# Unit 25 as three single-pass products, whole-unit low halves and an earlier mean in a two-layer decoder trunk

## Chip, core and metric

One NeuronCore of one Trainium2 chip runs the whole program. The metric is the device time of one execution in microseconds (us). The kernel before took 326.81 us (median of 3 runs, 326.73 to 327.3).

## What is computed

256 tokens of width 1024 pass through two residual layers. The change lies in layer 0:

```
def pool_conv_layer(x, norm_g, w_in, pool_w, pool_scale, conv_w, conv_b, cn_g, cn_b, w_out):
    h = rms_norm(x, norm_g)
    proj = jnp.einsum('bsd,de->bse', h, w_in)
    a, bv, bg, z = jnp.split(proj, [A_W, A_W + B_W, A_W + 2 * B_W], axis=-1)
    pooled = multiscale_pool(a.reshape(B, S, POOL_GROUPS, POOL_CH))
    ya = jnp.einsum('bsgc,gce->bsge', pooled, pool_w).reshape(B, S, A_W) * pool_scale
    u = bv * jax.nn.sigmoid(bg)
    u = lax.conv_general_dilated(u, conv_w[:, None, :], ...) + conv_b   # 31 causal taps
    yb = jax.nn.silu(layer_norm(u, cn_g, cn_b))
    y = jnp.concatenate([ya, yb], axis=-1) * jax.nn.silu(z)
    return jnp.einsum('bse,ed->bsd', y, w_out)          # x = x + this
```

Layer 1 is causal attention with a gate and its own two projections; nothing in its code changes. All inputs and outputs are float32.

## The kernel before

Channels lie on the 128 partitions, tokens on the free axis. The weights come as 49 units of 128 x 2048 float32 (1 MB each), loaded by SP into a ring of four slots (`raw`); unit n goes into slot n % 4 once unit n - 4 has been used up there. PE works through the units in order. Units 0 to 15 and 17 to 20 are layer 0's input projection, 16 is the pooling map, 21 to 24 (`OA`) and 25 to 28 (`OB`) are the two halves of layer 0's output projection, 29 to 32 (`Z1`) begin layer 1.

A unit is multiplied in one of two ways. In a **native** unit the float32 operands go to PE as they are; each of the 16 products of 256 columns is then two passes in the trace. Any other unit is cut: ACT copies each half (128 x 1024) rounded into `w_hi` (`cut_hi`, L466), DVE subtracts that from the raw half into `w_lo` (`cut_lo`, L750), and PE makes three single passes for a product (`product`, L1087 to L1089): high by high, high by low, low by high. Four units (`ADDED`) get their low part another way: ACT writes minus the high half into `w_lo` (L469), and a DMA issued by POOL adds the raw half to it (L431). The activations are split into high and low in the same way.

`w_hi` and `w_lo` have three slots in rotation, and a fourth that unit 22 uses first and the split activations `yb_hi` and `yb_lo` of the `OB` units afterwards.

While PE goes through units 1 to 20, DVE and ACT also make the 31 taps of the convolution, by a plan that the program works out in advance: for each unit n a list of taps (L864 one tile on DVE, L868 the addition of a product that ACT made at L557 or L537). In each such slot DVE first cuts the low halves of unit n + 2, then does its taps. After the last taps the order around the change is this:

- DVE folds the eight channel tiles to one for the layer norm's mean (L881, three instructions); PE multiplies that by a matrix of ones (L1213) in the middle of unit 23, at the place that `MEAN_AT` names: unit index, half, product.
- DVE subtracts the mean (L888), ACT squares (L474), DVE folds (L775), PE sums (L1167) in unit 24, at the place that `SUM2_AT` names.
- ACT takes the root (L478), DVE inverts it (L781), normalises (L931), ACT applies silu (L618), DVE gates with silu(z) (L936). The result `yb` is read by unit 25 as float32, and by units 26 to 28 in high (L625) and low (L941) parts.
- PE does units 25 and 26, then `closing` takes units 27 and 28 together, product row by product row, and counts each of four PSUM banks off as it is finished (`bank_closed`), so that DVE can add the residual (L969).

Each wait is a count on a semaphore; an engine executes its instructions strictly in the order in which they are written.

```
NATIVE = frozenset((0, 9, 16, 23, 25))
MEAN_AT = 2, 0, 5
SUM2_AT = 3, 0, 2
...
dve.wait_ge(hi_cut, 2 * s + half + 1)     # cut_lo: each half waits for its own high half
```

Of the kernel before, what the change touches and what calls it, by code (L numbers as in the profile page):

```python
# [17 lines left out]
F32 = mybir.dt.float32  # L18
F32R = mybir.dt.float32r
ALU = mybir.AluOpType  # L20
# [32 lines left out]
O1 = [45 + i for i in range(4)]  # L53
NU = 49

NATIVE = frozenset((0, 9, 16, 23, 25))
EARLY_ADDED = (10,)
ADDED = EARLY_ADDED + (21, 22, 24)
SPARE = 22
WARM = 12  # L60
RAW = 4
# [17 lines left out]
    return sum(1 for m in range(n) if m not in NATIVE)  # L79


def low_cuts(n):

    return sum(1 for m in range(n) if m not in NATIVE and m not in ADDED)


CUTS = [n for n in range(NU) if n not in NATIVE]
# [154 lines left out]
CONV_PLAN, TILE_DONE, PRODUCT_USED, LATE_FROM, FOLDED = conv_plan()  # L242


MEAN_AT = 2, 0, 5
SUM3_AT = 5
SUM2_AT = 3, 0, 2
EARLY = (BG[0],), (Z1[0], Z1[1], Z1[2])


def hybrid_trunk(nc, xT, w, vec, const, out):
    with ExitStack() as ctx:
# [3 lines left out]
        def sem(name):  # L256
            return ctx.enter_context(nc.semaphore(name))
# [80 lines left out]
        hi_cut, lo_cut = sem("hi_cut"), sem("lo_cut")  # L338
        minus_hi = sem("minus_hi")
        lo_added = [[sem(f"lo_added{n}{half}") for half in range(2)] for n in ADDED]  # L340
        unit_done = sem("unit_done")
        first_square, sq_ready, folded = sem("first_square"), sem("sq_ready"), sem("folded")
        rms_sum = sem("rms_sum")
# [25 lines left out]
        def column(c, n=1):  # L369
            return V_[:, c:c + n]  # L370
# [19 lines left out]
        @block.sync  # L390
        def _(sp):
            for i in range(2):
                sp.dma_start(X[:, 4 * i:4 * i + 4, :], xT[:, 4 * i:4 * i + 4, :]).then_inc(x_in[i], 16)
            for n in range(NU):
                m = n - RAW
                if m >= 0:
                    if m in NATIVE:
                        sp.wait_ge(unit_done, m + 1)
                    elif m in ADDED:
                        for half in range(2):  # L400
                            sp.wait_ge(lo_added[ADDED.index(m)][half], 16)
                    else:
                        sp.wait_ge(lo_cut, 2 * low_cuts(m) + 2)
                sp.dma_start(raw[:, n % RAW, :], w[stored_at(n), :, :]).then_inc(raw_in[n % RAW], 16)
                if n == 3:
                    sp.dma_start(C_[:, :], const).then_inc(const_in, 16)
            for m in range(4):
                sp.wait_ge(x_updated, 4 + m + 1)
                sp.dma_start(out[:, 2 * m:2 * m + 2, :], X[:, 2 * m:2 * m + 2, :]).then_inc(stored, 16)
            sp.wait_ge(stored, 64)  # L410
# [3 lines left out]
        def _(pool):  # L414
# [30 lines left out]
            for n in ADDED:  # L445
                if n not in EARLY_ADDED:
                    added_low(n)

            for r in range(8):
                pool.wait_ge(qk_ss, r + 1)  # L450
# [6 lines left out]
        def _(act):  # L457
            def cut_hi(n, parts=(0, 1)):

                if n >= NU or n in NATIVE:  # L460
                    return
                act.wait_ge(raw_in[n % RAW], 16 * (n // RAW + 1))
                if slot_free(n):
                    act.wait_ge(unit_done, slot_free(n))
                for half in parts:
                    nc.scalar.copy(halves(w_hi, cut_slot(n), half), halves(raw, n % RAW, half)).then_inc(hi_cut, 1)  # L466
                    if n in ADDED:
                        act.wait_ge(hi_cut, 2 * cut_index(n) + half + 1)
                        nc.scalar.mul(halves(w_lo, cut_slot(n), half), halves(w_hi, cut_slot(n), half).bitcast(F32),  # L469
                                      -1.0).then_inc(minus_hi, 1)  # L470
# [133 lines left out]


            act.wait_ge(ya_ready, 4)
            cut_hi(OB[1])
            for m in range(4):
                act.wait_ge(centred, m + 1)
                square(1, m, V)  # L610
            prime(ACT.Sqrt)
            cut_hi(OB[0])
            take_root(bank[2], 2)
            prime(ACT.Silu)
            for m in range(5):
                for c in (2 * m, 2 * m + 1) if m < 4 else ():
                    act.wait_ge(normed, c + 1 if m == 0 else 2 * m + 2)
                    nc.scalar.activation(V[:, c, :], V[:, c, :], ACT.Silu, bias=column(CBETA + c),  # L618
                                         scale=column(CG + c)).then_inc(swished, 1)
                if m >= 3:  # L620
                    cut_hi(OB[2], (m - 3,))
                if m >= 1 and OB[m - 1] not in NATIVE:
                    act.wait_ge(yb_ready, 2 * m)
                    act.wait_ge(unit_done, released(SPARE))
                    nc.scalar.copy(yb_hi[:, 2 * m - 2:2 * m, :], SZ[:, KD + 2 * m - 2:KD + 2 * m, :]).then_inc(ybhi_ready, 1)  # L625
            for n in range(OB[3], Z1[1]):
                cut_hi(n)

# [111 lines left out]

        @block.vector
        def _(dve):
            def cut_lo(n, parts=(0, 1)):

                if n >= NU or n in NATIVE or n in ADDED:
                    return
                s = cut_index(n)
                for half in parts:
                    dve.wait_ge(hi_cut, 2 * s + half + 1)
                    nc.vector.tensor_tensor(halves(w_lo, cut_slot(n), half), halves(raw, n % RAW, half),  # L750
                                            halves(w_hi, cut_slot(n), half).bitcast(F32), ALU.subtract).then_inc(lo_cut, 1)
# [146 lines left out]
            for n in range(1, OA[0] + 1):  # L898
# [5 lines left out]
                    value = bank[m % 4][:, :].rearrange("p (c t) -> p c t", c=2)  # L904
                    nc.vector.tensor_tensor(U[:, 2 * i:2 * i + 2, PAD:PAD + S], value, SG2, ALU.mult).then_inc(u_ready, 1)
                if n < OA[0] and n != A[3]:
                    cut_lo(n + 2)
                if m in A:
                    window_sums(m - A[0])
                if m in ZA:  # L910
# [4 lines left out]
                                            YP[:, 2 * i:2 * i + 2, :], ALU.mult).then_inc(ya_ready, 1)  # L915
                taps(n)
                if n == A[3]:
                    cut_lo(n + 2)
# [4 lines left out]

            centre()
            fold(1, 0, 4)
            cut_lo(OB[1], (0,))
            take_inverse(2)
            dve.wait_ge(sq_ready, 8)

# [9 lines left out]
            def low_yb(m):  # L939
                dve.wait_ge(ybhi_ready, pairs_cut(OB, m + 1))  # L940
                nc.vector.tensor_tensor(yb_lo[:, 2 * m:2 * m + 2, :], SZ[:, KD + 2 * m:KD + 2 * m + 2, :],  # L941
                                        yb_hi[:, 2 * m:2 * m + 2, :].bitcast(F32), ALU.subtract).then_inc(yblo_ready, 1)

            dve.wait_ge(sz_ready, 8)
            assert OB[0] in NATIVE
            normalise(0, 1)
            normalise(1, 2)
            gate_yb(0, 1)
            normalise(2, 4)
            gate_yb(1, 2)  # L950
            normalise(4, 6)
            gate_yb(2, 4)
            normalise(6, 8)
            low_yb(1)
            cut_lo(OB[1], (1,))
            for m in (2, 3):
                gate_yb(2 * m, 2 * m + 2)
                cut_lo(OB[2], (m - 2,))
                low_yb(m)
            for n in range(OB[3], Z1[1]):  # L960
                cut_lo(n)

# [120 lines left out]
        def _(pe):  # L1083
# [149 lines left out]

            for i in range(2):
                n = OB[i]
                if n not in NATIVE:
                    pe.wait_ge(yblo_ready, pairs_cut(OB, i + 1))
                for kt in range(2):
                    if n in NATIVE:
                        pe.wait_ge(yb_ready, 2 * i + kt + 1)  # L1240
# [5 lines left out]
            def closing(units, y, first_tile, acc, ready):  # L1246

                pe.wait_ge(ready[0], ready[1])
                for n in units:
                    assert n not in NATIVE  # L1250
                    arrived(n, 1)
                for m in range(KD):
                    for u, n in enumerate(units):
                        for kt in range(2):
                            last = out_product(n, kt, m, y, first_tile + 2 * u + kt, acc, False, u == len(units) - 1 and kt == 1)
                        if m == KD - 1 and u == 0 and len(units) == 2:
                            last.then_inc(unit_done, 1)
                    if m % 2 == 1 and m < KD - 1:
                        last.then_inc(bank_closed, 1)
                last.then_inc(unit_done, 1)  # L1260

            closing(OB[2:], (yb_hi, yb_lo), 4, 4, (yblo_ready, pairs_cut(OB, 4)))


            for n in Z1:
# [190 lines left out]
```

## Time and profile before

| | us |
|---|---|
| median of 3 runs | 326.81 |
| the profiled execution's own time | 326.94 |
| span of its trace | 325.1 |
| PE busy (2238 instructions) | 320.4 (99% of the span) |
| DVE busy (484) | 261.6 (80%) |
| ACT busy (440) | 236.8 (73%) |
| POOL busy (58) | 51.1 (16%) |

Busy time is the time in which an engine executed something. PE's instructions overlap in the pipeline, so its pace is read from the distance between starts, not from the duration of one. Between the profiled time and the span lie 1.84 us around the program; the profiled execution is 0.13 us above the median.

### The profile page before, as it was taken

To read this page: it belongs to the slowest core of one execution; us is meant where nothing else is said; L and a number is where in the kernel's file an instruction comes from. 1 tells how busy PE (TensorE), PEld (TensorE's weight loads), DVE (VectorE), ACT (ScalarE), POOL (GpSimd) and SP (SyncE) were. 2 spreads that over 40 slices of the span, in tenths; PEclk is the share of its full clock that TensorE was granted. 3 is DMA by queue.
4 is the path that set the end of the run, shared out by engine and by line. 5 is a ranking of instruction groups with operands and counts; after the bars stand their busy time and mean duration, and the time that the engine had idled before them with its cause. 6 is when DMAs were issued, how large, how long until landed. Compare 5 with 4: busy or idle time off the path is not lost.

```text
span 325.1 us, 5846 instructions
## 1 busy us (share of the span) xinstructions
PE 320.4 (99%) x2238; PEld 294.2 (90%) x2238; DVE 261.6 (80%) x484; ACT 236.8 (73%) x440; POOL 51.1 (16%) x58
## 2 busy tenths in 40 slices
PE   8999999999999999999999999999999999999995
PEld 8899999999999999998999999988877777778885
DVE  2799989999999999998895899746555877758533
ACT  4787999997999998997766588434666767566630
POOL 0040024422225112211000000004500231400000
PEclk9999999999999999999999999999999999999999
DMA  7988478979999599986639234871645323200003
GB/s 267 419 325 335 139 255 231 203 150 344 339 331 221 100 369 346 211 268 132 255 134 422 94 132 144 355 276 31 227 138 188 129 97 119 109 2 0 2 1 131
DMA packets 12844, 64.80 MB, mean 199 GB/s; under 512 B 1424, under 2 KB 1552, under 8 KB 6544
## 3 DMA queue, kind: packets, MB, share of 16 engines
q1 hardware_dynamic: 8064, 53.78, 44.3%
q0 software_dynamic: 4608, 10.49, 17.4%
q8 instruction: 18, 0.29, 0.3%
q10 hardware_dynamic: 144, 0.15, 0.2%
q14 instruction: 10, 0.08, 0.1%
HBM read 52.88 MB, written 1.05 MB: 166 GB/s over the span
## 4 chain that ended last, share of the span: by engine, by line
PE 99%; DVE 0%; POOL 0%; issue 0%; POOLq 0%
PE bank L1087 27%; PE bank L1088 26%; PE bank L1089 26%; PE bank L1147 4%; PE bank L1121 4%; PE bank L1198 2%; PE bank L1302 2%; PE bank L1329 2%; PE bank L1315 2%; PE bank L1155 2%; PE bank L1167 1%; PE bank L1281 1%; DVE X L969 0%; PE bank L1213 0%; POOL ones L415 0%
## 5 line engine op out<-in xcount | busy, mean ns | idle before, releaser
L750 DVE TENSOR_TENSOR w_lo<-raw,w_hi 128x1024 fp32r<-128x1024 f32 x80 | 95.1, 1220 | 15.1 <-ACT w_hi L466 14.8
L466 ACT CAST w_hi<-raw 128x1024 fp32r<-128x1024 f32 x88 | 88.5, 1047 | 5.7 <-PE bank L1089 4.1
L1087 PE MATMUL bank<-h_hi,w_hi 128*128 128x256 f32 x304 | 86.6, 285 | 0.0
L1089 PE MATMUL bank<-h_hi,w_lo 128*128 128x256 f32 x304 | 86.0, 283 | 0.0
L1088 PE MATMUL bank<-h_lo,w_hi 128*128 128x256 f32 x304 | 86.0, 283 | 0.0
L1088 PEld LDWEIGHTS bank<-h_lo,w_hi 128*128 128x128 f32 x304 | 58.3, 192 | 0.1
L1087 PEld LDWEIGHTS bank<-h_hi,w_hi 128*128 128x128 f32 x304 | 58.3, 192 | 0.1
L1089 PEld LDWEIGHTS bank<-h_hi,w_lo 128*128 128x128 f32 x304 | 58.3, 192 | 0.0
L1087 PE MATMUL bank<-ya_hi,w_hi 128*128 128x256 f32 x160 | 46.9, 293 | 0.0
L1089 PE MATMUL bank<-ya_hi,w_lo 128*128 128x256 f32 x160 | 45.2, 283 | 0.0
L1088 PE MATMUL bank<-ya_lo,w_hi 128*128 128x256 f32 x160 | 45.2, 282 | 0.0
L864 DVE SCALAR_TENSOR_TENSOR scratch<-scratch,params 128x256 f32<-128x256 f32 x104 | 42.6, 477 | 0.2
L1087 PE MATMUL bank<-w_hi,h_hi 128*128 128x512 f32 x96 | 39.2, 408 | 0.0
L1088 PE MATMUL bank<-w_lo,h_hi 128*128 128x512 f32 x96 | 37.6, 391 | 0.0
L1089 PE MATMUL bank<-w_hi,h_lo 128*128 128x512 f32 x96 | 37.5, 391 | 0.0
L557 ACT ACTIVATE scratch<-scratch,params 128x256 f32<-128x256 f32 x80 | 33.7, 502 | 0.5 <-DVE scratch L868 0.5
L440 POOL DMA_DIRECT2D side_v<-side_ring x24 | 21.1, 907 | 73.9 <-ACT side_ring L537 52.9
L1087 PEld LDWEIGHTS bank<-ya_hi,w_hi 128*128 128x128 f32 x160 | 30.6, 191 | 2.0 <-issue 1.7
L1088 PEld LDWEIGHTS bank<-ya_lo,w_hi 128*128 128x128 f32 x160 | 30.6, 191 | 0.1
L1089 PEld LDWEIGHTS bank<-ya_hi,w_lo 128*128 128x128 f32 x160 | 30.6, 191 | 0.0
L868 DVE TENSOR_TENSOR scratch<-scratch 128x512 f32<-128x512 f32 x40 | 26.2, 684 | 0.4
L1087 PEld LDWEIGHTS bank<-w_hi,h_hi 128*128 128x128 f32 x96 | 18.0, 188 | 5.6 <-issue 2.3
(107 smaller groups left out, 507.8 us busy)
## 6 DMA issues: line engine op xcount, KB each, us to landing
raw<-w SPq DMA_DIRECT2D x49, 1024.0 KB, 6.3
side_v<-side_ring POOLq DMA_DIRECT2D x24, 256.0 KB, 7.1
w_lo<-raw POOLq DMA_DIRECT2D x8, 512.0 KB, 7.4
X<-xT SPq DMA_DIRECT2D x2, 512.0 KB, 5.3
out<-X SPq DMA_DIRECT2D x4, 256.0 KB, 2.6
consts<-const SPq DMA_DIRECT2D x1, 290.0 KB, 13.6
params<-vec ACTq DMA_DIRECT2D x1, 149.0 KB, 5.0
```

Source lines behind the costliest of these rows:

```text
L440: pool.dma_start(side_v[:, pair, item % 2, :, :], side_home(pair, item), accum_op=ALU.add).then_inc(side_added[pair][item % 2], 16)
L466: nc.scalar.copy(halves(w_hi, cut_slot(n), half), halves(raw, n % RAW, half)).then_inc(hi_cut, 1)
L557: last = nc.scalar.mul(product_home(product)[:, i, :], U[:, c, k:k + S], column(CW + TAPS * c + k))
L750: nc.vector.tensor_tensor(halves(w_lo, cut_slot(n), half), halves(raw, n % RAW, half), halves(w_hi, cut_slot(n), half).bitcast(F32), ALU.s ...
L864: nc.vector.scalar_tensor_tensor(V[:, c, :], U[:, c, k:k + S], column(CW + TAPS * c + k), V[:, c, :], ALU.mult, ALU.add).then_inc(tap, 1)
L868: nc.vector.tensor_tensor(V[:, c:c + 2, :], V[:, c:c + 2, :], product_home(product), ALU.add).then_inc(tap, 1)
L1087: nc.tensor.matmul(dst, wh, ah, start=start, stop=False, skip_group_check=True)
L1088: nc.tensor.matmul(dst, wh, al, start=False, stop=False, skip_group_check=True)
L1089: return nc.tensor.matmul(dst, wl, ah, start=False, stop=stop, skip_group_check=True)
L1121: last = nc.tensor.matmul(dst, wr, (H if n else H0)[:, k, :], start=start, stop=stop, skip_group_check=True)
L1147: return nc.tensor.matmul(dst, wr, SZ[:, (KD if n in OB else 0) + tile, :], start=start and m % 2 == 0, stop=stop, skip_group_check=True)
L1155: nc.tensor.matmul(bank[7][:, 0:P], ones[:, :], ones[:, :], start=True, stop=True, skip_group_check=True)
```

## The change

Unit 25 leaves the set of native units. Its first low half is made by ACT and an added DMA on POOL's queue, its second by DVE; its activations are split too. For the units 3 to 20 that DVE cuts, one subtraction of 128 x 2048 takes the place of two of 128 x 1024, and waits for both high halves. The mean and the sum of squares each stand two products earlier in PE's order. The high and low parts of the first two `yb` tiles are made one tile at a time. Unit 26 is cut later on ACT and DVE, one half after the other. The last two `OB` units are taken bank by bank, first unit 27's four products for the bank and then unit 28's.

```
-NATIVE = frozenset((0, 9, 16, 23, 25))
+NATIVE = frozenset((0, 9, 16, 23))
+HALF_ADDED = 25
-MEAN_AT = 2, 0, 5
+MEAN_AT = 2, 0, 3
-SUM2_AT = 3, 0, 2
+SUM2_AT = 3, 0, 0
...
@@ SP: slot of unit 25 for unit 29
-                        sp.wait_ge(lo_cut, 2 * low_cuts(m) + 2)
+                        if m == HALF_ADDED:
+                            sp.wait_ge(half_added, 16)
+                        sp.wait_ge(lo_cut, low_cuts(m, 1))
@@ POOL, after the last added unit
+            n = HALF_ADDED
+            pool.wait_ge(minus_hi, 2 * len(ADDED) + 1)
+            pool.dma_start(halves(w_lo, cut_slot(n), 0).bitcast(F32), halves(raw, n % RAW, 0),
+                           accum_op=ALU.add).then_inc(half_added, 16)
@@ ACT, cut_hi
-                    if n in ADDED:
+                    if n in ADDED or n == HALF_ADDED and half == 0:
@@ ACT, after the gated ya
-            cut_hi(OB[1])
+            cut_hi(OB[0], (0,))
             for m in range(4):
                 act.wait_ge(centred, m + 1)
                 square(1, m, V)
+            cut_hi(OB[0], (1,))
             prime(ACT.Sqrt)
-            cut_hi(OB[0])
             take_root(bank[2], 2)
             prime(ACT.Silu)
+            cut_hi(OB[1], (0,))
...
+                if m == 0:
+                    high_yb(0, 1)
+                    high_yb(1, 2)
+                if m == 1:
+                    cut_hi(OB[1], (1,))
                 if m >= 3:
                     cut_hi(OB[2], (m - 3,))
+                if m >= 2:
+                    high_yb(2 * m - 2, 2 * m)
@@ DVE
+            def cut_lo_whole(n):
+                if n in NATIVE or n in ADDED:
+                    return
+                dve.wait_ge(hi_cut, 2 * cut_index(n) + 2)
+                nc.vector.tensor_tensor(w_lo[:, cut_slot(n), :], raw[:, n % RAW, :], w_hi[:, cut_slot(n), :].bitcast(F32),
+                                        ALU.subtract).then_inc(lo_cut, 2)
...
-                    cut_lo(n + 2)
+                    cut_lo_whole(n + 2)
...
-            cut_lo(OB[1], (0,))
+            cut_lo(OB[0], (1,))
             take_inverse(2)
...
@@ PE
-                    pe.wait_ge(lo_cut, 2 * low_cuts(n) + half + 1)
+                elif n == HALF_ADDED and half == 0:
+                    pe.wait_ge(half_added, 16)
+                else:
+                    pe.wait_ge(lo_cut, low_cuts(n, half))
...
+                    pe.wait_ge(yblo_ready, kt + 1 if i == 0 else 3)
...
-            closing(OB[2:], (yb_hi, yb_lo), 4, 4, (yblo_ready, pairs_cut(OB, 4)))
+            for b in range(4):
+                for u, n in enumerate(OB[2:]):
+                    if b == 0:
+                        pe.wait_ge(yblo_ready, 4 + u)
+                    for kt in range(2):
+                        if b == 0:
+                            arrived(n, kt)
+                        for m in (2 * b, 2 * b + 1):
+                            last = out_product(n, kt, m, (yb_hi, yb_lo), 4 + 2 * u + kt, 4, False, u == 1 and kt == 1)
+                    if b == 3 or u == 1:
+                        last.then_inc(unit_done if b == 3 else bank_closed, 1)
```

The order on DVE changes at the cuts of units 19 and 20 and after the root. First the end of the taps, before; the two rows of L750 are the low halves of units 19 and 20:

```order
79 L750 TENSOR_TENSOR w_lo<-raw,w_hi 128x1024 x2
80 L914 TENSOR_TENSOR scratch<-scratch 128x512
81 L864 SCALAR_TENSOR_TENSOR scratch<-scratch,params 128x256 x6
82 L861 TENSOR_TENSOR scratch<-scratch,side_v 128x512
83 L914 TENSOR_TENSOR scratch<-scratch 128x512
```

The same place after the change:

```order
79 L768 TENSOR_TENSOR w_lo<-raw,w_hi 128x2048
80 L942 TENSOR_TENSOR scratch<-scratch 128x512
81 L892 SCALAR_TENSOR_TENSOR scratch<-scratch,params 128x256 x6
82 L889 TENSOR_TENSOR scratch<-scratch,side_v 128x512
83 L942 TENSOR_TENSOR scratch<-scratch 128x512
```

Only the size of the subtraction differs there; nothing is moved past it, and the taps that follow are the same.

DVE after the inverse of the root, before (L931 normalise, L936 gate, L941 low part of yb, L750 low half of a unit: 26, 27, 27, then 28 and 29):

```order
102 L931 TENSOR_TENSOR scratch<-scratch,rinv 128x256 x2
103 L936 TENSOR_TENSOR scratch<-scratch 128x256
104 L931 TENSOR_TENSOR scratch<-scratch,rinv 128x512
105 L936 TENSOR_TENSOR scratch<-scratch 128x256
106 L931 TENSOR_TENSOR scratch<-scratch,rinv 128x512
107 L936 TENSOR_TENSOR scratch<-scratch 128x512
108 L931 TENSOR_TENSOR scratch<-scratch,rinv 128x512
109 L941 TENSOR_TENSOR w_lo<-scratch,w_hi 128x512
110 L750 TENSOR_TENSOR w_lo<-raw,w_hi 128x1024
```

And after the change (L959 normalise, L964 gate, L969 low part of yb, L778 low half of a unit, here 26 twice):

```order
102 L959 TENSOR_TENSOR scratch<-scratch,rinv 128x256 x2
103 L964 TENSOR_TENSOR scratch<-scratch 128x256 x2
104 L969 TENSOR_TENSOR w_lo<-scratch,w_hi 128x256
105 L959 TENSOR_TENSOR scratch<-scratch,rinv 128x512
106 L969 TENSOR_TENSOR w_lo<-scratch,w_hi 128x256
107 L778 TENSOR_TENSOR w_lo<-raw,w_hi 128x1024
108 L964 TENSOR_TENSOR scratch<-scratch 128x512
109 L959 TENSOR_TENSOR scratch<-scratch,rinv 128x512
110 L778 TENSOR_TENSOR w_lo<-raw,w_hi 128x1024
111 L969 TENSOR_TENSOR w_lo<-scratch,w_hi 128x512
112 L959 TENSOR_TENSOR scratch<-scratch,rinv 128x512
```

Two low parts of one tile and both halves of unit 26 now stand between the gates, and the last normalise comes behind them.

PE around the mean, before (L1147 products of unit 23, L1213 the mean):

```order
966 L1147 MATMUL bank<-scratch,raw 128x256 x6
967 L1213 MATMUL bank<-scratch,ones 128x256
968 L1147 MATMUL bank<-scratch,raw 128x256 x10
```

And after the change:

```order
966 L1179 MATMUL bank<-scratch,raw 128x256 x4
967 L1245 MATMUL bank<-scratch,ones 128x256
968 L1179 MATMUL bank<-scratch,raw 128x256 x12
```

The mean stands behind four products of unit 23 in place of six.

## Rows read from the trace of the kernel before

**Rows 1.** The page: busy time, and the chain that ended last by engine.
```profile
PE 320.4 (99%) x2238; PEld 294.2 (90%) x2238; DVE 261.6 (80%) x484; ACT 236.8 (73%) x440; POOL 51.1 (16%) x58
...
PE 99%; DVE 0%; POOL 0%; issue 0%; POOLq 0%
```

**Rows 2.** Timeline of PE, units 24 to 26: start, duration, instruction, count.
```profile
159.20 0.28 PE L1089 MATMUL bank<-ya_hi,w_lo 128*128 128x256 f32 x1
159.32 7.07 PE L1147 MATMUL bank<-scratch,raw 128*128 128x256 f32 x32
166.04 0.47 PE L1087 MATMUL bank<-w_hi 128*128 128x256 f32 x1
166.34 0.28 PE L1088 MATMUL bank<-w_lo,w_hi 128*128 128x256 f32 x1
```

**Rows 3.** Stretches: length, busy PE, PEld, DVE, ACT, POOL (instructions), clock, DMA share, GB/s.
```profile
60.00:104.00 44.00, 44.00 (x343) 43.17 (x343) 43.10 (x72) 41.38 (x82) 13.10 (x16) 1.00 1.01 273
104.00:134.00 30.00, 30.00 (x227) 29.17 (x227) 29.83 (x57) 28.09 (x49) 6.25 (x8) 1.00 0.90 258
```

**Rows 4.** Timeline of DVE, cuts of units 19 and 20; idle time before it in brackets.
```profile
115.17 2.36 DVE L750 TENSOR_TENSOR w_lo<-raw,w_hi 128x1024 fp32r<-128x1024 f32 x2 [0.17 <-ACT w_hi L466]
117.44 1.89 DVE L868 TENSOR_TENSOR scratch<-scratch 128x512 f32<-128x512 f32 x3
...
120.71 2.36 DVE L750 TENSOR_TENSOR w_lo<-raw,w_hi 128x1024 fp32r<-128x1024 f32 x2
122.99 0.68 DVE L914 TENSOR_TENSOR scratch<-scratch 128x512 f32<-128x512 f32 x1
```

**Rows 5.** Timeline of ACT: pooling results, then the high halves of units 19 and 20.
```profile
111.16 3.03 ACT L602 ACTIVATE scratch<-bank,params 128x256 f32<-128x256 f32 x8 [0.43 <-PE bank L1198]
114.03 2.04 ACT L466 CAST w_hi<-raw 128x1024 fp32r<-128x1024 f32 x2
...
119.61 2.02 ACT L466 CAST w_hi<-raw 128x1024 fp32r<-128x1024 f32 x2
```

**Rows 6.** Timeline of DVE, cuts of units 5 and 7.
```profile
30.59 2.36 DVE L750 TENSOR_TENSOR w_lo<-raw,w_hi 128x1024 fp32r<-128x1024 f32 x2
...
42.91 2.36 DVE L750 TENSOR_TENSOR w_lo<-raw,w_hi 128x1024 fp32r<-128x1024 f32 x2 [1.08 <-ACT w_hi L466]
```

**Rows 7.** Timeline of ACT: high halves of unit 5, last pair's first taps.
```profile
29.52 1.98 ACT L466 CAST w_hi<-raw 128x1024 fp32r<-128x1024 f32 x2
...
60.62 1.08 ACT L569 ACTIVATE scratch<-scratch,params 128x256 f32<-128x256 f32 x2
```

**Rows 8.** Timeline of DVE: first low part of ya, mean's folds.
```profile
132.53 0.68 DVE L895 TENSOR_TENSOR ya_lo<-scratch,ya_hi 128x512 fp32r<-128x512 f32 x1
...
145.24 2.41 DVE L881 TENSOR_TENSOR scratch<-scratch 128x1024 f32<-128x1024 f32 x3 [0.23 <-DVE scratch L868]
```

**Rows 9.** Timeline of PE: start of unit 21, unit 23 with the mean, sum in 24.
```profile
133.99 0.28 PE L1087 MATMUL bank<-ya_hi,w_hi 128*128 128x256 f32 x1
...
145.51 2.75 PE L1147 MATMUL bank<-scratch,raw 128*128 128x256 f32 x12
148.10 0.59 PE L1213 MATMUL bank<-scratch,ones 128*128 128x256 f32 x2
...
154.11 0.70 PE L1167 MATMUL bank<-scratch,ones 128*128 128x256 f32 x2
```

**Rows 10.** Groups of PE's weight loads, ya by w_lo: mean ns of one.
```profile
L1089 PEld LDWEIGHTS bank<-ya_hi,w_lo 128*128 128x128 f32 x160 | 30.6, 191 | 0.0
```

**Rows 11.** Timeline of ACT: the root, released by the sum.
```profile
154.85 0.47 ACT L478 ACTIVATE root<-bank,eps 128x256 f32<-128x256 f32 x1 [1.08 <-PE bank L1167]
```

**Rows 12.** Timeline of DVE: first gate of yb, low halves of unit 28.
```profile
158.24 0.42 DVE L936 TENSOR_TENSOR scratch<-scratch 128x256 f32<-128x256 f32 x1 [0.33 <-ACT scratch L618]
...
168.35 2.35 DVE L750 TENSOR_TENSOR w_lo<-raw,w_hi 128x1024 fp32r<-128x1024 f32 x2
```

**Rows 13.** DMA issues on POOL's queue: count, KB each, median us to landing.
```profile
w_lo<-raw POOLq DMA_DIRECT2D x8, 512.0 KB, 7.4
```

More of the change, by code:

```diff
@@ L79, in cut_index, with low_cuts @@
     return sum(1 for m in range(n) if m not in NATIVE)
-def low_cuts(n):
-    return sum(1 for m in range(n) if m not in NATIVE and m not in ADDED)
+def low_cuts(n, half):
+    whole = sum(2 for m in range(n) if m not in NATIVE and m not in ADDED)
+    return whole + half + 1 - (n > HALF_ADDED or n == HALF_ADDED and half == 1)
 CUTS = [n for n in range(NU) if n not in NATIVE]
@@ L340, in hybrid_trunk @@
         lo_added = [[sem(f"lo_added{n}{half}") for half in range(2)] for n in ADDED]
+        half_added = sem("half_added")
         unit_done = sem("unit_done")
@@ L610, in _, with high_yb @@
                 square(1, m, V)
+            cut_hi(OB[0], (1,))
             prime(ACT.Sqrt)
-            cut_hi(OB[0])
             take_root(bank[2], 2)
             prime(ACT.Silu)
+            cut_hi(OB[1], (0,))
+            def high_yb(a, b):
+                act.wait_ge(yb_ready, b)
+                nc.scalar.copy(yb_hi[:, a:b, :], SZ[:, KD + a:KD + b, :]).then_inc(ybhi_ready, 1)
+            act.wait_ge(unit_done, released(SPARE))
             for m in range(5):
@@ L619, in _ @@
                                          scale=column(CG + c)).then_inc(swished, 1)
+                if m == 0:
[3 more added lines that the diff above has]
+                    cut_hi(OB[1], (1,))
                 if m >= 3:
                     cut_hi(OB[2], (m - 3,))
[L622 to L625, printed above, removed]
+                if m >= 2:
+                    high_yb(2 * m - 2, 2 * m)
             for n in range(OB[3], Z1[1]):
@@ L917, in _ @@
                 if n == A[3]:
-                    cut_lo(n + 2)
+                    cut_lo_whole(n + 2)
                 if n == OA[0]:
@@ L937, in gate_yb, with low_yb @@
                                         V[:, a:b, :], ALU.mult).then_inc(yb_ready, b - a)
[L939 to L942, printed above, removed]
+            def low_yb(a, b, copies):
+                dve.wait_ge(ybhi_ready, copies)
+                nc.vector.tensor_tensor(yb_lo[:, a:b, :], SZ[:, KD + a:KD + b, :], yb_hi[:, a:b, :].bitcast(F32),
+                                        ALU.subtract).then_inc(yblo_ready, 1)
             dve.wait_ge(sz_ready, 8)
-            assert OB[0] in NATIVE
             normalise(0, 1)
@@ L948, in _ @@
             gate_yb(0, 1)
+            gate_yb(1, 2)
+            low_yb(0, 1, 1)
             normalise(2, 4)
-            gate_yb(1, 2)
+            low_yb(1, 2, 2)
+            cut_lo(OB[1], (0,))
+            gate_yb(2, 4)
             normalise(4, 6)
-            gate_yb(2, 4)
+            cut_lo(OB[1], (1,))
+            low_yb(2, 4, 3)
             normalise(6, 8)
-            low_yb(1)
-            cut_lo(OB[1], (1,))
             for m in (2, 3):
@@ L958, in _ @@
                 cut_lo(OB[2], (m - 2,))
-                low_yb(m)
+                low_yb(2 * m, 2 * m + 2, m + 2)
             for n in range(OB[3], Z1[1]):
@@ L1235, in _ @@
                 n = OB[i]
-                if n not in NATIVE:
-                    pe.wait_ge(yblo_ready, pairs_cut(OB, i + 1))
                 for kt in range(2):
-                    if n in NATIVE:
-                        pe.wait_ge(yb_ready, 2 * i + kt + 1)
+                    pe.wait_ge(yblo_ready, kt + 1 if i == 0 else 3)
                     arrived(n, kt)
@@ L1244, in _ @@
                 last.then_inc(unit_done, 1)
[L1246 to L1260, printed above, removed]
-            closing(OB[2:], (yb_hi, yb_lo), 4, 4, (yblo_ready, pairs_cut(OB, 4)))
+            for b in range(4):
[9 more added lines that the diff above has]
+                        last.then_inc(unit_done if b == 3 else bank_closed, 1)
             for n in Z1:
```

## The prediction

> **What bounds the kernel now.** I read the page first: PE is busy for 99% of the span, and the chain that ended last is 99% PE [rows 1]. So a change gains only what it takes out of PE's instruction stream, and loses whatever it makes PE wait. Second, the timeline of PE gives its pace: a single-pass product starts every 0.12 us, and unit 25, native, takes from 159.32 to 166.04; the pass after it is followed 0.30 later in place of 0.12 [rows 2]. Third, the stretches: the clock stands at 1.00, the higher of its two levels (2.4 GHz), and beside PE, DVE is almost as full, 43.10 of 44 us and 29.83 of 30 up to the end of the taps [rows 3]. DVE makes the mean that PE needs in unit 23, so DVE's timeline is where a wait would come from.
>
> **The change, part by part.**
>
> *Unit 25.* Native it costs 6.72 from its first pass to the next unit's, and 0.18 more by the slow step behind it: 6.90 [rows 2]. As a cut unit it has 48 passes of 0.12: 5.76. PE's stream loses **1.14 us**. Bounds of this: 1.0 if the slow step is no part of it, 1.2 with the rounding of the starts.
>
> *Whole low halves.* Fifteen units (3 to 8, 11 to 15, 17 to 20) have two subtractions joined. Two halves take 2.28 (120.71 to 122.99 [rows 4]). Three operations of 512 columns stand (1.89 - 0.68) / 2 = 0.605 apart [rows 4], so 512 columns more are 0.535, and a whole unit is 1.14 + 1.07 = 2.21: 0.07 less. Fifteen times is 1.0 us of DVE, all of it hidden behind PE, worth something only if the mean comes sooner. Against it, the joined one waits for both high halves. For unit 19 DVE starts its first half at 115.17, after waiting 0.17 for ACT [rows 4]; ACT's second half ends at 114.03 + 2.04 = 116.07 [rows 5]. ACT has worked without a gap since PE's pooling products released it at 111.16 [rows 5], so that end does not move forward. The whole subtraction starts at about 116.11, with 0.04 from release to start (the sum's end, 154.11 + 0.70, to the root at 154.85 [rows 9, 11]), and ends 2.21 later at 118.32; what stood at 117.44 is **0.88 late**. For unit 20 ACT's second half ends at 119.61 + 2.02 = 121.63 [rows 5], DVE arrives at about 121.6, and nothing is won back: the row of 122.99 goes to 123.88. From there to the last fold DVE has no idle time but 0.23 of its own, and every instruction there stays as it is, so the lateness passes on whole.
>
> It can be more than that. Unit 5 is the first case: both halves start at 30.59 [rows 6], ACT's second ends at 29.52 + 1.98 = 31.50 [rows 7], which makes DVE 0.88 late with no idle time to take it back but the 1.08 ahead of unit 7 [rows 6]. ACT itself waits for DVE's u before the first taps of the last pair (60.62 [rows 7]); these go later, with them the next high halves, and DVE then waits for these. Each later cut pays back 0.07 only. So at unit 19 DVE can come with more than 0.88 of its own. I take **1.1**, with ends 0.88 (units 19 and 20 alone) and 1.5 (one more such wait, two thirds of it kept).
>
> Here the Trainium skill speaks on both sides ("Perfetto Trace Analysis", Optimizing Scalar/DVE Operations). It puts about 60 ns of overhead on each DVE operation in SBUF and advises larger operations where the engine is saturated; by that alone DVE would be 15 x 60 ns = 0.9 us early (an estimate from that page), and nothing would be lost. The same section advises breaking instructions up where an engine that isn't saturated causes bubbles on others. The 0.07 of the rows agrees with the first; but the rows of units 19 and 20 show a producer half a unit behind, so I go by them.
>
> *First output unit.* Unit 21 needs the first low part of ya, which ends at 132.53 + 0.68 = 133.21 [rows 8]. At 1.1 late that is 134.31; a start of PE from a standstill costs 0.04 and a weight load of 0.19 [rows 10]: 134.54 against 133.99 [rows 9]. PE waits about 0.55. It isn't added, since the mean's wait is counted from the same plan.
>
> *The mean.* The last fold ends at 145.24 + 2.41 = 147.65 [rows 8], the mean's product runs at 148.10: 0.45 to spare. Twelve passes from 145.51 make 0.216 each [rows 9]; with four passes fewer ahead of it the mean is due at 148.10 - 0.86 = 147.24. Even with DVE as before, the fold would end after that. With 1.1 late it ends at 148.75, PE starts at 148.98: PE is **1.74 behind** its plan (1.52 and 2.14 at the ends).
>
> *From the mean to unit 25.* Before, the sum follows the mean by 6.01 (148.10 to 154.11 [rows 9]), with ACT held by two copies of unit 26. After, the sum's place in PE's order is 1.2 earlier but there are four passes more of unit 23 between: 0.43 + 12 x 0.43 + about 0.7 = 6.3, so DVE and ACT have as long as before; ACT's added copy and negation (1.05 each) fall into its wait for the mean. Nothing added. From the sum to unit 25 there are 15 products in place of 13: 5.21 + 0.72 = 5.93. The chain takes 158.24 + 0.42 - 154.11 = 4.55 to the first gate [rows 9, 12]; then 0.2 for a half of unit 26 cut ahead of silu on ACT, 0.3 because the second silu goes before the copy, 0.5 copy, 0.42 subtraction, 0.1 between them: 6.0 with PE's start. It just fits: **0.1**, ends 0 and 0.3. The added DMA is issued when ACT's negation is done, near 150, and lands 7.4 later [rows 13], 3 us before its use; its cover is that distance.
>
> *Units 26 to 28.* DVE ends unit 28's low halves 168.35 + 2.35 - 154.11 = 16.6 after the sum [rows 9, 12]. It gets two low parts (0.34 each) and a half of unit 26 (1.14) more, that is 18.4 without waits; ACT gets two halves of unit 26 and two small copies, about 2.7, and the last normalise now stands behind a low part that waits for ACT, so silu of the last tiles, the cut of unit 27 and DVE's subtraction of it all come later, by about 1.3. That makes 19.7. PE wants unit 28's second half at 5.93 + 2 x 5.76 + 6 products of 0.36 = 19.6, less 0.2 for the load. **0.4**, ends 0 and 0.8. The bank by bank order itself has the same products, and closes banks at the same products: 0. Later stages all wait for PE, and shift with it.
>
> Sum: 1.74 - 1.14 + 0.1 + 0.4 = +1.1 on the profiled 326.94, that is 328.0; this execution is 0.13 above the median, so the median would go from 326.81 to 327.9.
>
> **The rivals.** *Short waits.* DVE's lateness is the 0.88 of units 19 and 20 only, and the closing units are covered: 1.52 - 1.14 = +0.4, 327.2. For it: DVE idles 1.08 ahead of unit 7's cut [rows 6], which swallows what unit 5 loses. Against it: the stretch after that has hardly any idle time [rows 3]. *No wait at the mean: faster.* If the joined subtractions really bring DVE forward, the mean is in time and unit 25's 1.14 is kept: 325.7. It decides at the last fold: it must end by about 147.0, 0.65 earlier than before. For it: 1.0 us of DVE is saved on paper, and ACT could run ahead where its own waits for DVE shrink. Against it: ACT's stretch from 111.16 to 121.63 is released by PE [rows 5], so the cuts of units 19 and 20 can't come sooner. *The change does nothing that shows*, since the conversion is off the path: excluded by the chain, which is PE throughout [rows 1].
>
> **How the numbers follow.** A measurement of this kernel tells some 0.2% (0.65 us) from no change. The forecast gets 0.62, short waits 0.22, faster 0.13, something longer than all these 0.03. The predicted time is 327.9. Its own ends are +0.4 and +2.1 (1.52 or 2.14, less 1.14, and 0 or 1.1 behind it): 327.2 to 328.9. The range goes from 326.7, to take in short waits whose mean is nearly in time, to 328.9. Slower by over 0.2%: 0.62; within: 0.25 (short waits, and the low edge of the forecast); faster: 0.13.
>
> **What would show it.** Right: PE's timeline with a gap ahead of the mean and a smaller one at unit 21; the waits list with PE waiting for DVE's folds; DVE idle ahead of the cuts of units 19, 20 and 5; unit 25 as 48 passes of 0.12 in 5.76. Wrong: the last fold before 147.3, the mean's product at 147.24 without a gap, or a gap at unit 25 or in units 27 and 28 that is larger than the one at the mean.

## The result, and the profile after

The changed kernel takes 328.32 us (median of 5 runs, 328.16 to 328.84); the kernel before took 327.18 us in the same comparison (5 runs, 326.73 to 327.3). The ratio is 1.0044, 95% interval 1.003 to 1.0058: slower by 0.4%, some 1.4 us (1.0 to 1.9). The forecast was 327.9 us, slower by 1.1. The profiled execution took 328.32 us with a span of 326.4, against 326.94 and 325.1.

The page of the kernel after, the rows that answer to [rows 1]:

```profile
PE 319.7 (98%) x2254; PEld 294.0 (90%) x2254; DVE 262.2 (80%) x472; ACT 241.0 (74%) x445; POOL 51.9 (16%) x59
...
PE 89%; DVE 3%; DMA 3%; ACT 3%; issue 1%; POOL 0%; ACTq 0%; POOLq 0%
```

PE's busy time fell by 0.7 us although the kernel became longer, and the chain that ended last, 99% PE before, now runs for 9% through DVE, DMA and ACT. PE's waits say for what (us in total, times, longest):

```profile
PE bank L1117 <- DMA w_lo<-raw: 1.6, 1, 1.6
PE bank L1187 <- POOL eps L421: 1.0, 1, 1.0
PE bank L1117 <- DVE w_lo L778: 0.3, 1, 0.3
```

The 1.0 is the start of the program and stood there before too. New are a wait for an added transfer and one for DVE. The timeline of PE shows where (start, duration, instruction; idle time in brackets):

```profile
133.74 0.28 PE L1119 MATMUL bank<-h_hi,w_lo 128*128 128x256 f32 x1
135.59 0.35 PE L1117 MATMUL bank<-ya_hi,w_hi 128*128 128x256 f32 x1 [1.57 <-DMA w_lo<-raw]
...
147.18 1.89 PE L1179 MATMUL bank<-scratch,raw 128*128 128x256 f32 x8
148.95 0.67 PE L1245 MATMUL bank<-scratch,ones 128*128 128x256 f32 x2
...
155.00 0.61 PE L1199 MATMUL bank<-scratch,ones 128*128 128x256 f32 x2
...
160.85 0.28 PE L1117 MATMUL bank<-w_hi 128*128 128x256 f32 x1
...
166.49 0.28 PE L1119 MATMUL bank<-w_hi,w_lo 128*128 128x256 f32 x1
...
173.69 0.28 PE L1119 MATMUL bank<-w_hi,w_lo 128*128 128x256 f32 x1
174.23 0.35 PE L1117 MATMUL bank<-w_hi 128*128 128x256 f32 x1 [0.26 <-DVE w_lo L778]
...
174.89 0.28 PE L1119 MATMUL bank<-w_hi,w_lo 128*128 128x256 f32 x1
175.27 0.38 PE L1117 MATMUL bank<-w_hi 128*128 128x256 f32 x1
```

Passes start 0.12 apart, so unit 21 was due at 133.74 + 0.12 = 133.86 and began at 135.59: PE loses 1.73 us there. It then reaches the mean 13.36 later, at 148.95, without a wait that the page lists (the kernel before takes 148.10 - 133.99 = 14.11 [rows 9] with four passes more, so 14.11 - 0.86 = 13.25 for as many). Unit 25's 48 passes run from 160.85 to 166.49 + 0.12 = 166.61, that is 5.76. In unit 28 PE stands twice, 174.23 - 173.81 = 0.42 and 175.27 - 175.01 = 0.26, together 0.68.

DVE's timeline, at the cuts of units 19 and 20 (L768, to be held against [rows 4]), the first low parts of ya and the folds ([rows 8]), and the closing units:

```profile
116.55 2.28 DVE L768 TENSOR_TENSOR w_lo<-raw,w_hi 128x2048 fp32r<-128x2048 f32 x1
118.75 1.88 DVE L896 TENSOR_TENSOR scratch<-scratch 128x512 f32<-128x512 f32 x3
...
121.95 2.28 DVE L768 TENSOR_TENSOR w_lo<-raw,w_hi 128x2048 fp32r<-128x2048 f32 x1
124.15 0.68 DVE L942 TENSOR_TENSOR scratch<-scratch 128x512 f32<-128x512 f32 x1
...
133.69 1.29 DVE L923 TENSOR_TENSOR ya_lo<-scratch,ya_hi 128x512 fp32r<-128x512 f32 x2
...
146.40 2.41 DVE L909 TENSOR_TENSOR scratch<-scratch 128x1024 f32<-128x1024 f32 x3 [0.23 <-DVE scratch L896]
...
165.39 0.69 DVE L969 TENSOR_TENSOR w_lo<-scratch,w_hi 128x512 fp32r<-128x512 f32 x1 [0.54 <-ACT w_hi L629]
166.00 0.69 DVE L959 TENSOR_TENSOR scratch<-scratch,rinv 128x512 f32<-128x512 f32 x1
...
168.78 1.22 DVE L778 TENSOR_TENSOR w_lo<-raw,w_hi 128x1024 fp32r<-128x1024 f32 x1 [1.50 <-ACT w_hi L475]
...
172.87 2.35 DVE L778 TENSOR_TENSOR w_lo<-raw,w_hi 128x1024 fp32r<-128x1024 f32 x2
```

To compare traces I count from the moment at which unit 21 is due, 133.99 before and 133.86 now. The row behind unit 20's cut stood 11.00 us ahead of it (122.99 [rows 4]) and stands 9.71 ahead now (124.15): DVE is **1.29 us late**. The folds end at 146.40 + 2.41 = 148.81, 0.14 before the mean starts.

So two limits nearly coincide: the transfer holds PE at unit 21, and when PE comes to the mean the folds have only just ended. Which of the two costs the time, the one trace can't say. The transfer itself, in the view of DMA issues between 124.5 and 127 us (count, size, us from issue to landing), before:

```profile
w_lo<-raw POOLq DMA_DIRECT2D x1, 512.0 KB, 7.6
```

and after:

```profile
w_lo<-raw POOLq DMA_DIRECT2D x1, 512.0 KB, 10.4
```

Both were issued at nearly the same time (125.17 and 125.03). But SP loads unit 24 when unit 20's low cut frees its buffer, and that load was issued at 123.1 before and at 124.26 after; it landed at 131.30 before, 6.1 us into the transfer, and at 132.92 now, 7.9 us into it.

### The profile page after: what moved, and what is told of

Same layout as the page of the kernel before. It is cut to its first block, busy times and chain, and to the rows that moved or that the text cites. A ratio compares the mean times of both kernels' runs of the same rounds, so it can differ in the third digit from the quotient of the medians.

```text
span 326.4 us, 5891 instructions
## 1 busy us (share of the span) xinstructions
PE 319.7 (98%) x2254; PEld 294.0 (90%) x2254; DVE 262.2 (80%) x472; ACT 241.0 (74%) x445; POOL 51.9 (16%) x59
## 3 DMA queue, kind: packets, MB, share of 16 engines
HBM read 52.88 MB, written 1.05 MB: 165 GB/s over the span
## 4 chain that ended last, share of the span: by engine, by line
PE 89%; DVE 3%; DMA 3%; ACT 3%; issue 1%; POOL 0%; ACTq 0%; POOLq 0%
PE bank L1117 24%; PE bank L1118 23%; PE bank L1119 23%; PE bank L1153 4%; DMA w_lo<-raw 3%; PE bank L1179 2%; PE bank L1230 2%; PE bank L1326 2%; PE bank L1353 2%; PE bank L1339 2%; PE bank L1187 2%; DVE w_lo L778 1%; PE bank L1199 1%; PE bank L1305 1%; ACT w_hi L475 1%
## 5 line engine op out<-in xcount | busy, mean ns | idle before, releaser
L475 ACT CAST w_hi<-raw 128x1024 fp32r<-128x1024 f32 x90 | 90.5, 1046 | 1.1 <-PE bank L1119 1.1
L778 DVE TENSOR_TENSOR w_lo<-raw,w_hi 128x1024 fp32r<-128x1024 f32 x51 | 61.0, 1219 | 12.6 <-ACT w_hi L475 12.5
L768 DVE TENSOR_TENSOR w_lo<-raw,w_hi 128x2048 fp32r<-128x2048 f32 x15 | 34.3, 2284 | 3.8 <-ACT w_hi L475 3.8
```

The costliest lines, as they stand in the source:

```text
L768: nc.vector.tensor_tensor(w_lo[:, cut_slot(n), :], raw[:, n % RAW, :], w_hi[:, cut_slot(n), :].bitcast(F32), ALU.subtract).then_inc(lo_cut, 2)
```

## The experiments

Three theories. **A**: the joined subtractions wait for the second high half and make DVE late; everything else is a consequence. **B**: the added transfer of unit 21 lands late, and this alone costs the time. **C**: the mean was moved too far forward. All ratios are to the kernel before.

**Halves again, all else as changed.** At both places in DVE's loop:

```diff
-                    cut_lo_whole(n + 2)
+                    cut_lo(n + 2)
```

> The change with the fifteen joined subtractions taken back to halves; all else as changed. Theory A (the joined subtractions make DVE late, and that sets both the wait at unit 21 and the mean): the last fold ends near 147.6, the wait of PE at unit 21 (1.76 us behind its plan in the changed kernel) goes, the mean due at 147.2 waits about 0.6, the closing units still about 0.5: 328.3 - 1.8 + 0.6 = 327.1. Rival B (the added transfers as such are slow with one more of them, not because of DVE): the wait at unit 21 stays, 328.3. Rival C (the earlier place of the mean is the loss): the mean waits more than 1 us whatever DVE does, 328 or more.

Measured: 327.5 us (327.25 to 327.93, 11 runs), ratio 1.0008 (0.9996 to 1.002). The waits of PE:

```profile
PE bank L1117 <- DVE w_lo L778: 0.5, 1, 0.5
PE bank L1245 <- DVE scratch L909: 0.4, 1, 0.4
```

Unit 21 waits for nothing, its transfer lands in 7.7 us, and the mean waits 0.4. A holds in its mechanism; the time is 0.4 above the 327.1 that it gave, and unit 28 loses 0.90 where some 0.5 was expected. Of C there remains this 0.4.

**The joining alone, in the kernel before** (unit 25 native, the old closing): the same edit the other way round.

> The kernel before with the fifteen joined subtractions and nothing else: unit 25 native, mean and sum in their old places. Theory A: DVE's last fold ends near 148.8, PE waits at unit 21 and at the mean for about 0.95 us together, 327.0 + 0.95 = 328.0; where unit 21's transfer lands as late as in the changed kernel, the wait there can be 1.7 and the time 328.7. Rival C (the mean's place or unit 25 is the loss, the joining is free or a gain): 327.0 or less.

Measured: 329.26 us (328.19 to 329.71, 6 runs), ratio 1.0061 (1.0043 to 1.0078). PE, at the sum of squares:

```profile
156.68 0.70 PE L1175 MATMUL bank<-scratch,ones 128*128 128x256 f32 x2 [1.25 <-DVE scratch L783]
```

and ACT ahead of it, the two copies of unit 26:

```profile
150.74 1.99 ACT L466 CAST w_hi<-raw 128x1024 fp32r<-128x1024 f32 x2 [2.80 <-issue]
```

This is longer than either time that A gave. PE waits 1.05 us at unit 21, where the page names ya; but ya's low part ended at 133.88 + 0.68 = 134.56, and the transfer landed at 135.08, just ahead of PE's start at 135.22. And there is a second wait, which no theory had: ACT copies unit 26 ahead of the squares (at 152.63), and stood 2.80 us for it: its load landed at 150.67, against 148.10 before. The load could go out only when unit 22's second transfer had landed, at 143.85 against 140.90. The joining alone costs some 2 us, more than the whole change, in which unit 25's gain is set against it and unit 26 is cut behind the first squares.

**Unit 24's load kept behind unit 21's transfer**, in the changed kernel, on SP:

```diff
+                if n == 24:
+                    sp.wait_ge(lo_added[ADDED.index(21)][0], 16)
```

> The changed kernel, with one more wait: the load of unit 24 is issued only when the first added transfer of unit 21 has landed, so that the two do not share the DMA engines. Theory A with DVE's fold as the last limit: unit 21's transfer lands near 132.5 and PE's wait there falls from 1.76 to about 0.6 (DVE's low part of ya), but the wait moves to the mean, whose fold ends as late as before: unchanged, 328.3. Rival B (the late transfer alone is the loss): 1.2 less, 327.1.

Measured: 329.89 us (329.48 to 331.35, 6 runs), ratio 1.0091 (1.007 to 1.0111), outside of what either theory said. Unit 21's transfer, same view as above:

```profile
w_lo<-raw POOLq DMA_DIRECT2D x1, 512.0 KB, 5.2
```

So the load beside it was what made it slow. At unit 21 PE came 0.63 late in place of 1.73, as A said (about 0.6). But the loads of units 24 and 25 now lay beside unit 22's transfers, which took 11.1 and 12.4 us, and PE waited at unit 22 instead (2.16 us, shown in the last section). This run shows what delays the transfer; for what the delay costs it is inconclusive, since it moved the collision and did not remove it.

**Halves, and the last normalisation earlier.** On the version with halves:

```diff
+            normalise(6, 8)
             cut_lo(OB[1], (1,))
             low_yb(2, 4, 3)
-            normalise(6, 8)
```

> The version of halves, with the last normalise (tiles 6 and 7) placed ahead of unit 26's second low half and the low part of tiles 2 and 3, as it stood in the kernel before. Theory A with the closing wait caused by that order on DVE and ACT: the waits in units 27 and 28 (0.5) go, so 0.5 less than the version of halves: 326.6, and 0.4 less than the kernel before. Rival (the closing wait comes from the amount of DVE's work, or from the bank by bank order): no more than 0.1 less than the version of halves.

Measured: 326.51 us (326.05 to 326.68, 11 runs), ratio 0.998 (0.9971 to 0.9988): faster than both kernels, and 1.0 below the halves, where 0.5 was expected. The mean still waits, the closing units don't:

```profile
147.64 0.67 PE L1245 MATMUL bank<-scratch,ones 128*128 128x256 f32 x2 [0.39 <-DVE scratch L909]
```

**Which joined cuts?** Two kernels that share them out: units 19 and 20 alone joined, and the other thirteen alone.

```diff
+                    (cut_lo_whole if n in (17, 18) else cut_lo)(n + 2)
```

> The changed kernel with the low halves in pairs again (the version that measured 327.5 us, ratio 1.0008), only units 19 and 20 made whole. Late theory (the joined instruction that stands right ahead of the mean, where the second high half comes from a busy ScalarE, makes VectorE late): VectorE waits some 0.7 to 0.9 us for unit 19's second high half, the loads of units 23 and 24 are issued 0.6 to 1 us later, TensorE waits 0.4 to 1.5 us at unit 21, 328.0 to 328.5 us. Early theory (VectorE is late since the first joined units, whose second high half it waited 1.29 and 1.22 us for, and never makes it up): nothing is late at unit 19 but these two, 327.4 to 327.8 us.

```diff
+                    (cut_lo if n in (17, 18) else cut_lo_whole)(n + 2)
```

> The changed kernel with units 19 and 20 in pairs again, the other thirteen whole. Late theory: VectorE reaches unit 19 about as early as with pairs throughout, no wait at unit 21, 327.4 to 327.8 us. Early theory: VectorE reaches unit 19 some 0.8 us later than with pairs throughout, the loads of units 23 and 24 follow, unit 21 waits 0.5 to 1.6 us for its added transfer or for VectorE, 328.0 to 328.5 us.

Measured: 19 and 20 alone 328.11 us (328.02 to 328.4, 5 runs), ratio 1.0042 (1.0029 to 1.0054); the other thirteen alone 328.39 us (328.28 to 328.81, 5 runs), ratio 1.0051 (1.0038 to 1.0063). Each part costs what the whole costs. DVE, with 19 and 20 joined:

```profile
116.19 2.29 DVE L768 TENSOR_TENSOR w_lo<-raw,w_hi 128x2048 fp32r<-128x2048 f32 x1 [1.19 <-ACT w_hi L475]
...
123.96 0.68 DVE L942 TENSOR_TENSOR scratch<-scratch 128x512 f32<-128x512 f32 x1
```

and with the thirteen others joined:

```profile
31.63 2.29 DVE L768 TENSOR_TENSOR w_lo<-raw,w_hi 128x2048 fp32r<-128x2048 f32 x1 [1.28 <-ACT w_hi L475]
...
116.72 2.35 DVE L778 TENSOR_TENSOR w_lo<-raw,w_hi 128x1024 fp32r<-128x1024 f32 x2
...
124.47 0.68 DVE L942 TENSOR_TENSOR scratch<-scratch 128x512 f32<-128x512 f32 x1
```

Counted from unit 21's due time (134.00 and 134.02) DVE is 0.96 and 1.45 us late. Late and early theory are both true, and the two don't add: a DVE that comes late to unit 19 finds both high halves there and waits no more. What counts is the larger one. With the thirteen joined PE waits in two places, neither time for a transfer:

```profile
134.79 0.36 PE L1117 MATMUL bank<-ya_hi,w_hi 128*128 128x256 f32 x1 [0.62 <-DVE ya_lo L923]
...
149.27 0.67 PE L1245 MATMUL bank<-scratch,ones 128*128 128x256 f32 x2 [1.01 <-DVE scratch L909]
```

The transfer, issued at 125.19 and 9.3 us long, landed at 134.53; ya's low part ended later, at 134.01 + 0.68 = 134.69. This is what decides between A and B: the transfer is covered, and the time is not shorter.

**The changed kernel, joined, with the normalisation earlier.**

> The changed kernel with its whole units, but with the last normalisation ahead of unit 27's second low half and of the third low piece of yb. With pairs that move was worth 1.0 us (327.5 to 326.5). If the closing wait and the wait at unit 21 are apart from each other, TensorE still waits 1.3 to 1.8 us at unit 21, the 0.26 us wait and the gap behind it in the closing part go, and the time is 327.3 to 327.9 us. If the delay of VectorE reaches the closing part too, some of the wait stays there: 328.0 to 328.4 us.

Measured: 327.42 us (327.26 to 327.94, 11 runs), ratio 1.002 (1.0011 to 1.0029). The closing waits are gone; unit 21 and the mean still wait:

```profile
135.43 0.35 PE L1117 MATMUL bank<-ya_hi,w_hi 128*128 128x256 f32 x1 [0.99 <-DVE ya_lo L923]
...
149.40 0.67 PE L1245 MATMUL bank<-scratch,ones 128*128 128x256 f32 x2 [0.49 <-DVE scratch L909]
```

The two losses are apart from each other. The expected 1.3 to 1.8 at unit 21 was off, as that wait is now divided between unit 21 and the mean. At unit 21 the page names ya, but ya's low part ended at 134.13 + 0.68 = 134.81; the transfer landed at 135.30, and PE started 0.13 later, as it did in the changed kernel (135.46 and 135.59).

**Halves, normalisation earlier, and the mean one product later.**

```diff
-MEAN_AT = 2, 0, 3
+MEAN_AT = 2, 0, 4
```

> The version with pairs and the earlier normalisation (326.51 us, ratio 0.998), with the mean one product later, between its place before the change and its place after. If the 0.39 us that TensorE waits at the mean is simply lost there, the wait falls to 0 and the time to 326.1 to 326.3 us. If the mean sets the end of the chain of layer norm (root, inverse, first normalisation), what is saved at the mean comes back as a wait of 0.2 to 0.4 us at the sum of squares: 326.4 to 326.6 us.

Measured: 326.2 us (325.98 to 326.49, 11 runs), ratio 0.9975 (0.9963 to 0.9987). The mean no longer waits, and the sum of squares does:

```profile
153.62 0.70 PE L1199 MATMUL bank<-scratch,ones 128*128 128x256 f32 x2 [0.20 <-DVE scratch L803]
```

The wait is that of the second reading, the time that of the first. The traces, one of each version, speak for the second: from unit 21's due time to the first pass of unit 29, the first unit of layer 1, this version takes 48.73 us and the one before it 48.74, so nothing was gained there. The intervals of 0.998 and 0.9975 overlap. The version beats both kernels either way.

**Seven kernels in one sum.** "Late" is DVE's lateness behind unit 20's cut; "to the mean" is PE's delay there, from unit 21's due time and the 13.36 us that PE needs from unit 21 to the mean; "closing" is the standstill in unit 28 (in the last row, at the sum of squares). The sum takes off 1.14 for unit 25. "Trace" uses none of this: it is the time from unit 21's due time to the first pass of unit 29, less that of the kernel before. The first pass of unit 29 before, and then in the changed kernel:

```profile
183.50 0.28 PE L1087 MATMUL bank<-ya_hi,w_hi 128*128 128x256 f32 x1
```

```profile
184.73 0.28 PE L1117 MATMUL bank<-ya_hi,w_hi 128*128 128x256 f32 x1
```

That is 183.50 - 133.99 = 49.51 before and 184.73 - 133.86 = 50.87 after. From there to PE's last row every trace takes 137.6, so nothing is won or lost later; and that unit 21 is due at 133.83 to 134.57 in the different traces is left out by counting from there.

| kernel | late | to the mean | closing | sum | trace | measured (ratio - 1) x 326.9 |
|---|---|---|---|---|---|---|
| changed | 1.29 | 1.73 | 0.68 | +1.3 | +1.4 | +1.4 (1.0 to 1.9) |
| halves | 0.00 | 0.45 | 0.90 | +0.2 | +0.3 | +0.3 (-0.1 to 0.7) |
| 19, 20 joined | 0.96 | 1.40 | 0.90 | +1.2 | +1.2 | +1.4 (0.9 to 1.8) |
| thirteen joined | 1.45 | 1.89 | 0.69 | +1.4 | +1.5 | +1.7 (1.2 to 2.1) |
| joined, normalisation | 1.32 | 1.76 | 0 | +0.6 | +0.5 | +0.7 (0.4 to 0.9) |
| halves, normalisation | 0 | 0.45 | 0 | -0.7 | -0.8 | -0.7 (-0.9 to -0.4) |
| the same, mean later | 0 | 0 | 0.35 | -0.8 | -0.8 | -0.8 (-1.2 to -0.4) |

In every row the delay at the mean is 0.44 to 0.45 plus DVE's lateness (0 in the last, where the mean was put later), whether the page names a transfer, ya or the folds. That is theory A, in numbers. Counted with the 13.25 in place of the 13.36, each sum is 0.1 higher; all stay in their intervals. Two kernels are not in the table, because in them transfers cost time of their own: the joining alone lost 2.56 from unit 21 to unit 29, and the one with unit 24's load kept back 3.97. In the first the transfers are late because DVE is; in the second a load was moved onto them.

## Why the prediction was right

*Unit 25*, -1.14: the 5.76 of its 48 passes are there, and the sum of the halves with the earlier normalisation (0.45 - 1.14 = -0.7, measured -0.7) bears out the price, to some 0.2 (that trace shows -0.77).

*DVE's lateness*, 1.1 with ends 0.88 and 1.5: 1.29. Its two sources are the ones that were named, and each alone suffices: units 19 and 20 (0.88 forecast, 0.96 alone) and the early units (1.45 alone). But the base of the forecast, the 0.88 of units 19 and 20, did not come about in the changed kernel: there DVE had no idle time ahead of either cut (116.55 and 121.95 above), since it came later than ACT. All of its lateness is from earlier units. It stood ahead of unit 5, for 0.58 ahead of unit 11 (at 66.37), and ahead of unit 14:

```profile
31.48 2.30 DVE L768 TENSOR_TENSOR w_lo<-raw,w_hi 128x2048 fp32r<-128x2048 f32 x1 [1.29 <-ACT w_hi L475]
...
85.25 2.29 DVE L768 TENSOR_TENSOR w_lo<-raw,w_hi 128x2048 fp32r<-128x2048 f32 x1 [0.74 <-ACT w_hi L475]
```

Before there was no idle time at these three; unit 5 is in [rows 6], and units 13 and 14 read

```profile
80.96 4.63 DVE L750 TENSOR_TENSOR w_lo<-raw,w_hi 128x1024 fp32r<-128x1024 f32 x4
```

The row behind unit 14's cut stood 1.95 later than before (87.45 against 85.50), the one behind unit 20's 1.16 later: "one more such wait" was two more, and a part was paid back. That the size still came out near 1.1 is in part luck. The saving per joined cut is 0.08 by these rows (116.55 to 118.75 is 2.20, a pair takes 2.28) against 0.07. The Trainium skill ("Perfetto Trace Analysis", Optimizing Scalar/DVE Operations) has two rules here, larger operations for a saturated engine and smaller ones where an engine that isn't saturated causes bubbles elsewhere. The first would have made DVE early. By the runs above the smaller operations were the better ones, although by its busy time DVE is the first rule's case in this stretch (30.00 of 30 us busy after, as against 29.83 in [rows 3]).

*The mean*, PE 1.74 behind (1.52 to 2.14): 1.73 at unit 21, and 1.84 at the mean when counted as the prediction did (148.95 against 133.86 + 13.25 = 147.11). Part of this closeness is luck: lateness was 0.2 larger, and the mean starts 0.14 after the folds in place of 0.23.

*First output unit*, 0.55 for DVE's low part of ya: here the step failed. The low part came as forecast, 133.69 + 0.68 = 134.37 against 134.31. But PE waited until 135.59, for unit 21's added transfer. I followed DVE's lateness to its own products and not to the buffers that it frees: the loads of units 23 and 24 wait for the low cuts of 19 and 20, went out 1.2 to 1.3 us later, and slowed the transfer beside them from 7.6 to 10.4 us. The time did not suffer, as that wait was counted once, at the mean, and the mean would have stood at 148.81 + 0.15 = 148.96 without it.

*From the sum to unit 25*, 0.1: 160.85 - 155.00 = 5.85 against 5.93 of planned products: no wait, 0. The added transfer was hidden, as costed.

*Units 26 to 28*, 0.4 (0 to 0.8): 0.68. The mechanism is the one given, the last normalisation behind a low part that waits for ACT. DVE's rows above show it (165.39, then 166.00), and ACT's the next links, silu and the cut of unit 27:

```profile
164.76 0.60 ACT L629 CAST w_hi<-scratch 128x512 fp32r<-128x512 f32 x1
166.72 1.09 ACT L635 ACTIVATE scratch<-scratch,params 128x256 f32<-128x256 f32 x2 [1.36 <-DVE scratch L959]
167.72 1.03 ACT L475 CAST w_hi<-raw 128x1024 fp32r<-128x1024 f32 x1
```

Taking the normalisation out from behind it removed the waits in both versions (ratios 1.0044 to 1.002, 1.0008 to 0.998). The place was right, its size was 0.3 short; with the 0.1 that was not lost ahead of unit 25 the sum comes to +1.3 (+1.4 with the 1.84 at the mean), against +1.1 forecast and +1.4 measured.

*The rivals.* Short waits asked for a lateness of only 0.88 and a covered closing part; both failed. Faster asked for folds that end 0.65 earlier; they ended at 148.81 in place of 147.65, 1.16 later. Bank by bank order was costed at 0, and no run speaks against it; it wasn't tried alone.

*The signs.* Of the signs of being right, unit 25's passes and DVE's idle time ahead of unit 5 came; DVE's idle time ahead of units 19 and 20, a gap of PE ahead of the mean and a wait of PE for the folds did not. One sign of being wrong came: the loss in unit 28 (0.68) is larger than the gap at the mean (none). The loss was forecast at the mean with a smaller part of it at unit 21; in the changed kernel nearly all of it stood at unit 21, for a transfer. So the forecast was right in its cause, the joined cuts that make DVE late, and in its sum; it was not right in which of the cuts do it in this kernel, nor in where PE would stand.

## What to carry to other kernels

Joining two operations whose inputs arrive one after the other saves the overhead of one (0.08 us here) and puts the whole wait for the second input ahead of the first: check for each pair where the producer stands when the consumer arrives. Follow a late engine into the buffers that it frees, because the loads behind them will move onto other transfers. And when a trace names one wait, ask what would have ended just after it: here three different releasers were named for the same loss, and in two kernels (the joining alone, and the joined one with the normalisation earlier) the low part that was named had ended half a microsecond before the transfer that PE really waited for.

## What the runs showed of the hardware

A transfer of 512 KB that adds in place (POOL's queue) took 5.2 us from issue to landing where unit 24's load of 1 MB was issued only after it had landed, 7.6 where that load was issued 2.1 us ahead of it, and 10.4 where it was 0.8 us ahead. The distance alone doesn't give the time: with the thirteen units joined it was 0.6 us and the transfer took 9.3.

The other surprise was the price of a standstill of PE. With unit 24's load kept back, PE stood from 140.54 to 142.86, and its passes then started 0.21 apart in place of 0.12:

```profile
140.42 0.28 PE L1121 MATMUL bank<-ya_hi,w_lo 128*128 128x256 f32 x1
142.86 0.55 PE L1119 MATMUL bank<-ya_hi,w_hi 128*128 128x256 f32 x1 [2.16 <-DMA w_lo<-raw]
143.21 0.41 PE L1120 MATMUL bank<-ya_lo,w_hi 128*128 128x256 f32 x1
143.42 0.41 PE L1121 MATMUL bank<-ya_hi,w_lo 128*128 128x256 f32 x1
```

The stretches of that kernel (busy time by engine with instructions, granted clock, DMA share, GB/s):

```profile
136.00:140.00 4.00, 4.00 (x36) 4.00 (x35) 4.00 (x9) 3.02 (x8) 0.00 (x0) 1.00 1.04 247
...
145.00:146.00 1.00, 1.00 (x7) 1.00 (x7) 1.00 (x3) 1.00 (x3) 0.00 (x0) 0.50 1.03 197
146.00:147.00 1.00, 1.00 (x9) 1.00 (x9) 0.77 (x2) 0.97 (x2) 0.00 (x0) 0.91 0.59 111
```

The granted clock fell to 0.50, the lower of its two levels (1.2 GHz), and was back by 147. Fifteen passes from 142.86 to 146.19 took 3.33 in place of 15 x 0.12 = 1.8: a standstill of 2.32 us cost 1.5 us on top. Of six executions of that kernel two, with mean clocks of 0.995 and 0.993, took 331.2 and 331.35 us; the other four, at 0.997 to 1.0, took 329.48 to 330.12. In the changed kernel the standstill of 1.73 us left the clock at 1.00.
